# Where the slabs three ahead are split, the order of evictions in the mixers, and the root in the routing

## What is computed

```python
# first block
h = h + (sigmoid(ga + b_ga) * ya + sigmoid(gb + b_gb) * yb) @ w_out     # ga, gb: columns of n @ w_in
u = causal_conv_3(n @ w_up) + conv_b
h = h + (silu(u[:, :D_FF]) * u[:, D_FF:]) @ w_down                      # D_FF = 2816
# second block, layer l
a, u, v, cv, cg = split(rms_norm(x, norm1_g[l]) @ w_in[l])
ya = pool_mixer(a)              # mean over the last 2, 4, 8 or 16 rows, less a; then a product
yb = gmlp_mixer(u, v)
yc = conv_module(cv, cg)        # 31 taps
x = x + concat(ya, yb, yc) @ w_out[l]
h = rms_norm(x, norm2_g[l])     # x / root(mean square) * weight
l == 0:  x = x + swiglu(h)      # width 2816
l == 1:  logits = h @ router; top 2 of 8; x = x + sum of gate_e * swiglu_e(h)
```

## Time and profile before

| | us |
|---|---|
| runs | 1905.53, 1903.82, 1906.39 |
| median | 1905.53 |
| the profiled execution | 1903.46 |
| its span in the trace | 1901.6 |
| PE busy in the span | 1839.1 (97%) |
| DVE busy | 1487.9 (78%) |
| ACT busy | 1162.5 (61%) |

### The profile page before, as it was taken

One profiled execution on the slowest core, in us unless ns is written; L12 is line 12 of the kernel. 1 busy time (PEld: TensorE's weight loads), 2 busy tenths in 40 slices (PEclk: granted clock), 3 DMA queues, 4 the chain that ended last, 5 costly groups with the idle time before them and its releaser, 6 DMA issues.

```text
span 1901.6 us, 25922 instructions
## 1 busy us (share of the span) xinstructions
PE 1839.1 (97%) x10249; PEld 1598.6 (84%) x10249; DVE 1487.9 (78%) x1629; ACT 1162.5 (61%) x1101; POOL 56.0 (3%) x71
## 2 busy tenths in 40 slices
PE   7999898999989999999899999999999999999997
PEld 7988887999887999997788888888888888888885
DVE  6664567677795665596888889889889898998897
ACT  4445556555543444453677777777776776777765
POOL 0000000000320000140000000000000000000000
PEclk9999999999989999999999999999999999999998
DMA  9434333665461665454799999999999999999993
GB/s 324 144 97 133 130 137 109 227 203 188 129 194 45 206 213 196 144 180 148 251 370 379 362 345 366 361 374 360 346 370 367 369 364 343 363 368 365 374 359 121
DMA packets 258047, 495.70 MB, mean 261 GB/s; under 512 B 9625, under 2 KB 99455, under 8 KB 257919
## 3 DMA queue, kind: packets, MB, share of 16 engines
q1 hardware_dynamic: 253263, 489.04, 73.1%
q10 hardware_dynamic: 4656, 4.93, 0.8%
HBM read 492.89 MB, written 1.05 MB: 260 GB/s over the span
## 4 chain that ended last, share of the span: by engine, by line
PE 83%; DVE 8%; ACT 6%; issue 1%; DMA 1%; DVEq 0%; SPq 0%; ACTq 0%
PE bank L438 25%; PE bank L440 25%; PE bank L439 25%; DVE splitL L398 4%; ACT splitH L394 3%; PE bank L1790 1%; PE bank L2179 1%; PE bank L2110 1%; PE bank L1897 1%; DVE fb L1553 1%; DMA raw<-in_w_out 1%; DVE fb L1551 0%; PE bank L1199 0%; PE bank L2149 0%; PE bank L2148 0%
## 5 line engine op out<-in xcount | busy, mean ns | idle before, releaser
L398 DVE TENSOR_TENSOR splitL<-raw,splitH 128x2048 fp32r<-128x2048 f32 (+1 forms) x338 | 767.9, 2278 | 222.0 <-ACT splitH L394 211.4
L394 ACT ACTIVATE splitH<-raw 128x2048 fp32r<-128x2048 f32 (+1 forms) x338 | 640.8, 1902 | 164.9 <-PE bank L440 145.1
L438 PE MATMUL bank<-splitH,RBH 128*128 128x512 f32 x960 | 380.2, 396 | 2.6 <-DVE RBL L1565 1.1
L440 PE MATMUL bank<-splitH,RBL 128*128 128x512 f32 x960 | 374.4, 390 | 0.0
L439 PE MATMUL bank<-splitL,RBH 128*128 128x512 f32 x960 | 374.1, 390 | 0.0
L438 PE MATMUL bank<-RAH,splitH 128*128 128x256 f32 x1088 | 312.1, 287 | 12.4 <-DVE SG L1070 5.8
L439 PE MATMUL bank<-RAL,splitH 128*128 128x256 f32 x1088 | 308.3, 283 | 0.0
L440 PE MATMUL bank<-RAH,splitL 128*128 128x256 f32 x1088 | 308.2, 283 | 0.0
L438 PEld LDWEIGHTS bank<-RAH,splitH 128*128 128x128 f32 x1088 | 209.0, 192 | 16.5 <-ACT RAH L480 6.6
L438 PEld LDWEIGHTS bank<-splitH,RBH 128*128 128x128 f32 x960 | 180.4, 188 | 39.6 <-ACT RBH L1564 1.5
L440 PEld LDWEIGHTS bank<-splitH,RBL 128*128 128x128 f32 x960 | 180.2, 188 | 38.5
(11 more groups left out here) (324 smaller groups left out, 2249.7 us busy)
## 6 DMA issues: line engine op xcount, KB each, us to landing
raw<-in_moe_wg SPq DMA_DIRECT2D x71, 1024.0 KB, 6.2
raw<-in_moe_wu SPq DMA_DIRECT2D x71, 1024.0 KB, 6.6
raw<-in_moe_wd SPq DMA_DIRECT2D x69, 1024.0 KB, 6.6
rawx<-in_moe_wd SPq DMA_DIRECT2D x29, 1024.0 KB, 6.5
rawx<-in_moe_wu SPq DMA_DIRECT2D x28, 1024.0 KB, 6.8
rawx<-in_moe_wg SPq DMA_DIRECT2D x27, 1024.0 KB, 6.4
raw<-in_w_in SPq DMA_DIRECT2D x24, 1024.0 KB, 6.1
raw<-in_w_up SPq DMA_DIRECT2D x22, 1024.0 KB, 5.4
```

Of the source, the lines that this page charges most:

```text
L394: a = act.op(lambda e: e.activation(h[:, 0:size], r[:, 0:size], ACT.Copy), self.landed[n], over)
L398: d = dve.op(lambda e: e.tensor_tensor(l[:, 0:size], r[:, 0:size], h[:, 0:size].bitcast(F), ALU.subtract), self.landed[n], over, a)
L438: e.matmul(o, lh, rh, start=start, stop=False)
L440: return e.matmul(o, ll, rh, start=False, stop=stop)
```

## The change

- Gates: each slab is taken with the splits of two slabs ahead of it only, and the third is split behind the evictions of the slab (`W.ahead(2)` behind the release: one slab more has been taken by then, so it is the same slab).
- FFNs: the same for the up slabs, with `W.ahead` behind the eviction of the slab. The last step keeps one slab less ahead. In the FFN with convolution the value slab of the last step has no `W.ahead`.
- Mixers: `ma` is taken without splits ahead. Its two evictions into at_rows come first; then `scale_residual`, the change of table, and the splits up to two ahead. at_rows lies in a buffer of its own, 7 KB further on, and the eviction into py waits for `scale_residual`.
- Routing: the norm's root is no longer finished in `later`. X is multiplied by the weight alone, in four pieces of 128 x 512, each as soon as its part of X is there; the root is finished behind the selection and applied in the four evictions into tokH and the four steps of tokL.

```diff
@@ -1062,7 +1062,7 @@
         def fill_gates():
             for s in range(4):
                 for q, key in enumerate(("ga", "gb")):
-                    Wt = W.take(key)
+                    Wt = W.take(key, 2)
                     for m in range(2):
                         u = 2 * s + m
                         b = ps.take()
@@ -1071,6 +1071,7 @@
                             SG[:, u, q, :], banks[b][:, 0:256], R1[:, :], ALU.mult), t, attn_a.free)
                         ps.free[b] = [sg_t[u, q]]
                     W.release(Wt[3], t)
+                    W.ahead(2)
                     yield
 
         weave(attn_b(), fill_gates(), 0.8)
@@ -1238,12 +1239,14 @@
                 self.rows.added(1, d1)
                 self.rows.added(3, d3)
 
-            def later(self):
+            def later(self, root=True):
 
                 t = [self.turn(4 + k, b) for k, b in enumerate(self.spare)]
                 for k, b in enumerate(self.spare):
                     self.split(4 + k, b, t[k])
                 act.op(lambda e: e.activation(sm[:, 250:251], sm[:, 251:252], self.table), tzero)
+                if not root:
+                    return
                 self.r, self.tr = self.rows.finish(self.tp)
                 norm_r.append((self.r, self.tr))
                 D, r = self.D, self.r
@@ -1407,7 +1410,7 @@
         rs = at("rs", [128, 2, 256], ph + 48 * KB)
         sgc = at("sgc", [128, 3, 256], ph + 56 * KB)
         py = at("py", [128, 2, 256], ph + 59 * KB)
-        at_rows = at("at_rows", [128, 2, 256], ph + 61 * KB)
+        at_rows = at("at_rows", [128, 2, 256], ph + 68 * KB)
         diag = at("diag", [128, 31, 128], base + 112 * KB)
         rt = at("rt", [128, 8, 8], ph + 72 * KB)
         rtH = at("rtH", [128, 8, 8], ph + 72 * KB + 256, FR)
@@ -1518,7 +1521,7 @@
                         if i == 0:
                             bk, tt = early[which]
                         else:
-                            Wt = W.take(key, 3 if i < 10 else 2)
+                            Wt = W.take(key, 2 if i < 10 else 1)
                             bk = [ps.take(), ps.take()]
                             tt = [wstat(Wt, banks[bk[m]][:, 0:256], nAH, nAL, m, all8, True, True,
                                         ps.free[bk[m]], by=nn) for m in range(2)]
@@ -1536,6 +1539,8 @@
                                     tq = dve.op(lambda e, G=G, Y=Y, m=m, src=src: e.tensor_tensor(Y[:, m, :], G[:, m, :], src, ALU.mult),
                                                 tq, ev[0], gfree[i % 2])
                                 ev[which].append(tq)
+                            if i > 0:
+                                W.ahead(2 if i < 10 else 1)
                             continue
                         if i == 0:
                             continue
@@ -1558,6 +1563,8 @@
                         else:
                             ev[1] = dve.op(lambda e, G=G, V=V, Y=Y: e.tensor_tensor(
                                 Y[:, :, :], G[:, :, :], V[:, :, :], ALU.mult), last, ev[0], gfree[i % 2])
+                        if which == 0 or i < 10:
+                            W.ahead(2 if i < 10 else 1)
                     h = RBH[:, 512 * (i % 4):512 * (i % 4) + 512]
                     l = RBL[:, 512 * (i % 4):512 * (i % 4) + 512]
                     yf = Y[:, :, :].rearrange("p m t -> p (m t)")
@@ -1719,7 +1726,6 @@
                 some_taps(5)
 
 
-            txg = scale_residual() if l == 0 else None
             b = ps.take()
 
             def f(e, b=b):
@@ -1732,16 +1738,18 @@
                   evac(wsT[64:128, :, 64:128], bv[64:128, :, 64:128], t),
                   pool.op(lambda e: e.memset(wsT[64:128, :, 0:64], 0.0), t, tdiag)]
             ps.free[b] = tw[0:2]
-            act.op(lambda e: e.activation(sm[:, 250:251], sm[:, 251:252], ACT.Silu), tzero)
             ps.use(range(4, 8))
-            Wt = W.take("ma")
+            Wt = W.take("ma", 0)
             ta = []
-            row = put_r(lambda tb: at_rows[:, tb, :], ta, txg)
+            row = put_r(lambda tb: at_rows[:, tb, :], ta)
             for tb in range(2):
                 b = ps.take()
                 t = tstat(Wt, banks[b][:, 0:256], nAH, nAL, tb, all8, (0, 256), True, True, ps.free[b])
                 ps.free[b] = [row(tb, banks[b][:, 0:256], t)]
             W.release(Wt[3], t)
+            txg = scale_residual() if l == 0 else None
+            act.op(lambda e: e.activation(sm[:, 250:251], sm[:, 251:252], ACT.Silu), tzero)
+            W.ahead(2)
             some_taps(6)
 
 
@@ -1760,7 +1768,7 @@
                                         start=False, stop=True)
                     return last
                 tband = pe.op(f, ta, lcn, ps.free[b])
-                pooled.append(evac(py[:, m, :], banks[b][:, 0:256], tband))
+                pooled.append(evac(py[:, m, :], banks[b][:, 0:256], tband, txg))
                 ps.free[b] = [pooled[m]]
 
 
@@ -1959,7 +1967,7 @@
 
         iota, before, tie, eidx = c2[:, 0:128], c2[:, 128:256], c2[:, 256:320], c2[:, 320:328]
         ps.use(range(8))
-        lz.later()
+        lz.later(False)
         n7, tn = lz.n, [lz.tp]
         for q in engines:
             q.wait(fenced)
@@ -1976,7 +1984,9 @@
         lgT = at("lgT", [128, 256], ph + 12 * KB)
         t = act.op(lambda e, b=b: e.activation(lgT[0:8, :], banks[b][0:8, 0:256], ACT.Copy), t)
         ps.free[b] = [t]
-        trow = scale_rows(scr, None, tx, lg, tn)
+        txg = [dve.op(lambda e, tb=tb, h=h: e.tensor_tensor(
+            scr[:, tb, 512 * h:512 * h + 512], X[:, tb, 512 * h:512 * h + 512], grow[:, 512 * h:512 * h + 512],
+            ALU.mult), tx, lg, lz.rows.last[2 * tb + h]) for h in range(2) for tb in range(2)]
         b = ps.take()
 
         def f(e, b=b):
@@ -1985,11 +1995,9 @@
                                    ident[0:8, 0:8])
             return last
         t = pe.op(f, t, ps.free[b])
-        lgf = row_load(grow[:, :], w["final_g_2"], 1024, trow)
+        lgf = row_load(grow[:, :], w["final_g_2"], 1024, txg)
         tokH = RAH[:, :].rearrange("p (b d) -> p b d", b=2)
         tokL = RAL[:, :].rearrange("p (b d) -> p b d", b=2)
-        trh = [act.op(lambda e, o=o: e.activation(tokH[:, :, o], scr[:, :, o], ACT.Copy), trow)
-               for o in (slice(0, 512), slice(512, 1024))]
         L = rr[:, 0:16].rearrange("p (t e) -> p t e", t=2)
         gate = rr[:, 16:32].rearrange("p (t e) -> p t e", t=2)
         sel = rr[:, 32:48].rearrange("p (t e) -> p t e", t=2)
@@ -2012,6 +2020,10 @@
         t2 = dve.op(lambda e: e.tensor_tensor(rr[:, 128:256], rr[:, 128:256], rr[:, 256:384], ALU.add), t1, t2)
         t2 = dve.op(lambda e: e.tensor_reduce(sel, A4, AX, ALU.add), t2)
         tsel = dve.op(lambda e: e.tensor_scalar(sel, sel, 2.0, None, ALU.is_lt), t2)
+        lz.r, lz.tr = lz.rows.finish(tn)
+        trh = [[act.op(lambda e, o=o, tb=tb: e.activation(tokH[:, tb, o], scr[:, tb, o], ACT.Copy,
+                                                          scale=lz.r[:, tb:tb + 1]), txg, lz.tr[tb]) for tb in range(2)]
+               for o in (slice(0, 512), slice(512, 1024))]
         b = ps.take()
 
         def f(e):
@@ -2035,9 +2047,9 @@
         def behind_first_pick():
 
             for half, o in enumerate((slice(0, 512), slice(512, 1024))):
-                lrow.append(dve.op(lambda e, o=o: e.tensor_tensor(tokL[:, :, o], scr[:, :, o],
-                                                                  tokH[:, :, o].bitcast(F), ALU.subtract),
-                                   trow, trh[half]))
+                lrow.append([dve.op(lambda e, o=o, tb=tb: e.scalar_tensor_tensor(
+                    tokL[:, tb, o], scr[:, tb, o], lz.r[:, tb:tb + 1], tokH[:, tb, o].bitcast(F), ALU.mult,
+                    ALU.subtract), trh[half][tb]) for tb in range(2)])
 
         def behind_first_gather():
 
```

## The result

The changed kernel takes 1892.50 us (median of four runs, 1889.79 to 1893.75), the kernel before 1904.67 on the same chips: a ratio of 0.9935 with a 95% interval of 0.9917 to 0.9952, some 12.4 us won. The forecast was 1891, within 1885 to 1898. The profiled execution took 1892.46 us with a span of 1890.6, 11.0 less than before.

What follows compares the result with a forecast made beforehand. TensorE, busy 97% of the span, was taken as the bound, with some 62 us idle to win back. Terms 5.9 + 0.4 + 6.1 + 0.2 + 1.0 = 13.6 us gave 1889.9 by profile, 1891.9 by median; forecast 1891, range 1885 to 1898.

Steps and rivals of the forecast that it cites:

- Gates, 5.9: Gate slabs: SG evicted ahead of splitL ends PE's 5.75 us wait, a 1.35 us wait for BL comes; 5.9 us won.
- First mixers, 6.1: First layer's mixers: at_rows earlier, long product L1790 starts 4.7 us earlier and runs at full clock, 1.3 to 1.4 more.
- the first rival: The clock falls in the new gap before L1790, which stays at 15.0 us: 12.3 won, 1892.3; chance 0.19.
- FFNs, 0.4 won: Both FFNs: steady steps have slack; at the ends 0.5 us won in the first, 0.1 lost in the second.
- no new wait for splitL: Sign to look for in the FFNs' trace: PE gets no new wait for splitL; such a wait would show the prediction wrong.
- two stretches that may come or go: Half-clock stretches at L1897, 1.7 us each, that may shift with the moved phase; counted in the range 1885 to 1898.
- Second mixers, 0.2: Second layer's mixers: at_rows 0.6 us earlier, but L1790 starts at 848.35 instead of 848.58; 0.2 us won.
- Routing, 1.0: Routing: root moved behind the selection, rank ends at 906.3 instead of 907.9, Pm at 909.55 instead of 910.56; 1.0 us won.
- rival 2: The clock stays up in the routing where it falls now: 2.2 us more won, 1889; chance 0.13.
- Late splits, the rival on the slower side: FFNs: splits behind evictions come too late and PE waits at every such slab: 1932; chance 0.04.
- The table load: Mixers, rival 5: the moved table load holds ACT longer than its row, py 1.28 us later in both layers: 1893.6; chance 0.02.
- Rivals 3 and 6: 3: attention chain takes back gates' gain, 1893.7, chance 0.09; 6: queue order doesn't set these waits, no change, 1905, chance 0.05.

Runs made afterwards that it cites:

- the two sets: The changed kernel's two measurements against the kernel before: 1892.50 us (ratio 0.9935), and once more, unaltered, 1889.84 us (0.9926).
- the first set: The first measurement of the changed kernel, with all four parts, against the kernel before: 1892.50 us, ratio 0.9935.
- the gates' split in halves: Changed kernel with the gates' third split cut in two: splitH stays behind the evictions, splitL comes one step later; 1888.86 us, ratio 0.9922 to the kernel before.
- the second profile: Trace of the changed kernel run once more, unaltered, as base of the later versions: 1889.84 us, ratio 0.9926 to the kernel before.
- the first try: Changed kernel with splits reordered at the FFN loop's start and at both FFNs' ends: 1897.97 us, ratio 0.9959 to the kernel before.

## Why the prediction was right

The sum was 13.6 us; 12.4 and 14.1 (0.9926) were measured in the two sets. That the sum came so close is in part luck: its terms fared unequally, and their errors cancelled.

- **Gates, 5.9: right in its steps**, 6.0 by position and 5.9 by the part alone (4.0 to 7.8). BL was put at 196.4 and ended at 196.7, the new wait at 1.35 and was 1.61.
- **First mixers, 6.1: the waits right, the term for the clock wrong.** PE reached the long product 4.8 us earlier (4.7 predicted), py held it 2.13 (up to 2.3). The 1.3 to 1.4 for a full clock didn't come; 0.4 was lost instead. That term took the 15.0 us of one execution for the price of the old order. In the traces of the gates, the FFNs and the routing alone, which have the old order, the product took 13.58:

```profile
556.78 13.58 PE L1791 MATMUL bank<-hc,diag 128*128 128x256 f32 x62
```

  The slow product is the first rival's. Its price for the whole, 1892.3, is what the first set measured, and not the second (1889.84, with the product slow there too). Its reason holds only in part. Half clock followed the py wait in five of the seven traces that have that wait, both of the changed kernel among them, but not with the mixers' part alone nor with the gates' split in halves; it came in none of the three traces with the product in bank 3, where the wait is gone. And the gaps at 280 to 293, which the prediction set against this rival as they left the clock at 1.0, have a stretch at half clock among or behind them in eight of the fourteen traces.
- **FFNs, 0.4 won: the step that failed.** The "no new wait for splitL" was wrong: 1.3 were lost at the start and 0.1 won at the end (1.4 and 0.4 in the second profile). For a steady step the working holds: the changed kernel's up slab that ends at 378.4 (its matmuls start at 372.65, 48 at 0.12 each) is followed by a splitL that is done at 385.1, T + 6.7 where T + 6.4 was predicted, and that slab is read at T + 11.2. But I followed the steady step only. At the loop's start DVE still works off step 0, and the splitL that PE waits for ended 12.8 us behind its product:

```profile
328.89 0.69 DVE L1572 TENSOR_TENSOR RBL<-fb,RBH 128x512 fp32r<-128x512 f32 x1 [0.70 <-ACT RBH L1571]
329.50 2.28 DVE L398 TENSOR_TENSOR splitL<-raw,splitH 128x2048 fp32r<-128x2048 f32 x1
331.70 0.48 DVE L1556 SCALAR_TENSOR_TENSOR fb<-bank,prm,fb 128x255 f32<-128x255 f32 x1
...
336.18 2.29 DVE L398 TENSOR_TENSOR splitL<-raw,splitH 128x2048 fp32r<-128x2048 f32 x1 [2.57 <-ACT splitH L394]
```

  At the end the last slab came 0.9 later (0.6 predicted). X then held PE for 1.15 us or not at all, by whether the slab took 4.36 us or, at half clock, 5.96: a stretch ahead of a wait costs little, since it shortens the wait.
- **L1897, not in the sum: 1.7 won**, by luck. Before, this product ran at half clock in both layers (stretches at 597.6 and 884.3). In the first profile the first layer's has gone, in the second profile the second layer's. It lay in the range as "two stretches that may come or go", and it covered the FFNs' error.
- **Second mixers, 0.2: right.** at_rows' wait there fell from 1.1 to 0.6.
- **Routing, 1.0: 0.6 by position**, within its bounds. The rank ended where predicted and Pm 0.2 earlier than predicted; the half clock then lay over more of the gather (from 897.7 to 904.5), so rival 2 fell. Its time alone is within noise, so that it won anything rests on the traces.
- **Late splits, the rival on the slower side.** The run with the splits one slab later shows the point from which it decides: one slab later costs 0.92 us of waiting and 1.15 of time a step in the first FFN. That the median is back at that of the kernel before is half clock in part, as said there.
- **The table load** holds ACT no longer than its row: it begins at 547.89, lasts 1.28, and the next activation begins at 549.18. The drain that the Trainium skill ("ScalarE: Activation LUTs", "What ACT_TABLE_LOAD costs") adds to a change of table appears in none of the traces here: in all fourteen, each load but the kernel's first begins 0.02 us behind the activation ahead of it, and the next begins 0.01 behind the load, unless it waits for data of another engine.
- **Rivals 3 and 6** fell: BL ended 2.3 us earlier than before (196.7, not 198.97), and SG's wait and at_rows' went with their own parts alone.

What stays open: the four parts alone won 5.9, -0.4, 3.8 and -0.4, 8.9 us in all, the whole 12.4 to 14.1. The intervals (some 2 us either way for each) allow that difference. The traces offer a reason: up to the last 20 us, the kernel before spent 30.7 us at a granted clock of 0.50, the changed kernel 17.1 in both profiles, the gates alone 23.9, the FFNs alone 27.3, the mixers and the routing alone 30.7 each. Whether removing waits together makes the stretches rarer, or these few profiles fell so, isn't settled; each of these figures is that of one execution.

## What to carry to other kernels

Splits, table loads and evictions share queues in order: put first what frees the bank that another engine needs next, and then find what stands behind the moved work, since its wait comes back smaller at the next bank. Work through the first and the last step of a loop as well as the steady one; both waits that the prediction missed lay there. A wait for a bank can sometimes be removed without touching any order, by taking another bank. And the time of a stretch in one execution is not the price of an order, where the clock differs from one execution to the next.

## What the runs showed of the hardware that I had not expected

The same program with the same waits (py 2.13 us in both profiles, BL 1.61 in both) has its half-clock stretches behind other gaps from one execution to the next. L1905, behind a gap of 2.1 us, ran at 1.00 in one profile of the changed kernel and at 0.54 in the other. With the FFN's ends changed (the first try), executions fell into two groups 5 us apart, 1892.8 to 1893.0 at a mean granted clock of 0.993 and 1897.7 to 1898.3 at 0.989. A change of one or two microseconds can therefore be read from waits and positions in the trace before it can be read from the time.
